# Experts' output rows added to x's rows in DRAM by the scatter, with the gate applied before the down projection

## The reference

```python
def hier_moe(x, norm_g, w_rg, b_rg, w_re, b_re, w_gate, w_up, w_down):
    hf = rmsnorm(x, norm_g).reshape(B * L, D)
    ...
    gates = jnp.sum(jax.nn.one_hot(expert_idx, N_EXPERTS, dtype=jnp.float32) * top_w[..., None], axis=1)
    y = jnp.zeros((T, D), jnp.float32)
    for e in range(N_EXPERTS):
        act = jax.nn.silu((hf @ w_gate[e]).astype(jnp.float32)) * (hf @ w_up[e]).astype(jnp.float32)
        y = y + (act * gates[:, e:e + 1]).astype(x.dtype) @ w_down[e]
    return x + y.reshape(B, L, D).astype(x.dtype)
```

## Time and profile before

| | us |
|---|---|
| median of 3 runs | 897.34 |
| lowest and highest of the runs | 894.37 and 900.54 |
| the profiled execution | 895.55 |
| its span, from the first to the last instruction | 893.7 |
| TensorE busy | 833.2 |
| VectorE busy | 614.2 |
| ScalarE busy | 464.4 |
| GpSimd busy | 263.2 |

### The profile page before, as it was taken

How to read it: one execution, slowest core, us unless ns; L and a number is a source line. 1 busy time by engine, 2 the same in 40 slices (tenths; PEclk the granted TensorE clock), 3 DMA queues, 4 the chain that set the end, 5 groups by cost and what they waited for, 6 DMA issues and landing times.

```text
span 893.7 us, 12179 instructions
## 1 busy us (share of the span) xinstructions
PE 833.2 (93%) x4237; PEld 672.5 (75%) x4237; DVE 614.2 (69%) x962; ACT 464.4 (52%) x767; POOL 263.2 (29%) x211
## 2 busy tenths in 40 slices
PE   8999999999999999999899999999999899999930
PEld 6787788878857888887577778888787588888820
DVE  4335544755677999997644454656646899999937
ACT  4523342512447888885243433451234488888722
POOL 0024991340031332231000299525101223322200
PEclk9999999999999999999899999999999999999965
DMA  8622223246818899983744222230694598999445
GB/s 279 179 75 75 71 60 95 84 127 225 354 65 350 328 330 396 397 336 126 260 115 129 67 72 83 71 118 1 193 400 184 182 406 306 381 387 382 191 149 193
DMA packets 61215, 183.67 MB, mean 206 GB/s; under 512 B 15564, under 2 KB 17868, under 8 KB 52826
## 3 DMA queue, kind: packets, MB, share of 16 engines
q1 hardware_dynamic: 46202, 147.49, 46.3%
q0 software_dynamic: 11520, 27.28, 8.8%
q10 hardware_dynamic: 3440, 8.21, 2.4%
HBM read 168.20 MB, written 29.65 MB: 221 GB/s over the span
## 4 chain that ended last, share of the span: by engine, by line
PE 85%; DVE 6%; DMA 4%; ACT 2%; issue 1%; SPq 0%; POOLq 0%; ACTq 0%
PE ps L386 14%; PE ps L390 11%; PE ps L389 11%; PE ps L1131 10%; PE ps L1133 10%; PE ps L1132 10%; PE ps L388 3%; PE ps L1138 3%; PE ps L1311 2%; PE ps L1110 2%; PE ps L1303 2%; PE ps L1243 1%; DMA back<-y_d 1%; DMA hg<-xn_d,rowidx 1%; PE ps L1268 1%
## 5 line engine op out<-in xcount | busy, mean ns | idle before, releaser
L386 PE MATMUL ps<-wh,hT 128*128 128x512 f32 x480 | 194.5, 405 | 9.1 <-DVE lT L1587 3.1
L1645 DVE TENSOR_TENSOR gul<-wgu,eh 128x1024 fp32r<-128x1024 f32 x128 | 150.7, 1217 | 6.8 <-ACT eh L878 6.7
L390 PE MATMUL ps<-wh,lT 128*128 128x512 f32 x384 | 150.5, 392 | 0.0
L389 PE MATMUL ps<-wl,hT 128*128 128x512 f32 x384 | 150.4, 392 | 0.0
L1636 DVE SCALAR_TENSOR_TENSOR wl<-raw,gcol,wh 128x512 fp32r<-128x512 f32 x80 | 75.3, 945 | 87.7 <-ACT wh L851 87.4
L878 ACT ACTIVATE eh<-wgu 128x1024 fp32r<-128x1024 f32 x128 | 128.9, 1058 | 8.3 <-PE ps L1133 6.9
L386 PEld LDWEIGHTS ps<-wh,hT 128*128 128x128 f32 x480 | 90.9, 189 | 31.8 <-issue 8.1
L1131 PE MATMUL ps<-eh,hgTh 128*128 128x512 f32 x256 | 103.3, 403 | 2.5 <-DVE hgTl L1656 2.1
L1133 PE MATMUL ps<-eh,hgTl 128*128 128x512 f32 x256 | 100.6, 393 | 0.0
L1132 PE MATMUL ps<-gul,hgTh 128*128 128x512 f32 x256 | 100.4, 392 | 0.0
L851 ACT ACTIVATE wh<-raw,gcol 128x512 fp32r<-128x512 f32 x80 | 57.7, 723 | 66.6 <-PE ps L388 49.5
(11 more groups left out here) (198 smaller groups left out, 1527.7 us busy)
## 6 DMA issues: line engine op xcount, KB each, us to landing
wgu<-in_gate_up SPq DMA_DIRECT2D x64, 1024.0 KB, 10.2
wdn<-in_w_down SPq DMA_DIRECT2D x64, 512.0 KB, 9.9
raw<-in_w_in SPq DMA_DIRECT2D x80, 256.0 KB, 2.7
raw<-in_w_out SPq DMA_DIRECT2D x32, 256.0 KB, 3.4
back<-y_d SPq DMA_DIRECT2D x16, 512.0 KB, 6.8
xn_d<-xf ACTq DMA_DIRECT2D x10, 512.0 KB, 3.7
s<-in_state_ret POOLq DMA_DIRECT2D x8, 512.0 KB, 4.8
out_new_ret_sample<-s POOLq DMA_DIRECT2D x8, 512.0 KB, 4.8
```

The lines of the kernel that those rows point to most:

```text
L386: pe.matmul(out, both, w_h, start=first, stop=False)
L389: pe.matmul(out, both, w_l, start=False, stop=False)
L390: return pe.matmul(out, l[:, t * P:(t + 1) * P], w_h, start=False, stop=final)
L1645: ve.tensor_tensor(gu_pair(gul, gul3, e, s, p), gu_pair(wgu, wgu3, e, s, p), eh[p][:, :].bitcast(F32), ALU.subtract).then_inc(glo, 1)
```

## The change

The gate is applied to the activation, before the down projection, in the same VectorE instruction that multiplies by the up half; for this the gate of each slot is needed (`gslot`), which comes out of ten small matmuls (`slot_gates`) on the gates in three bf16 parts (`gate_parts`, VectorE, once a layer, at expert 0).

x's tiles are stored to DRAM (`x_d`) once a layer by SyncE, ahead of expert 3's weights. The scatter adds its rows to those of `x_d` (`compute_op=ALU.add`) and waits for the scatter before it, as two experts may have the same token. An empty slot of partition p goes to a spare row, TOK + p, of `x_d`, so that every scatter has 128 rows in range; the gather still leaves them out. One table of indices takes the place of two.

After the last scatter SyncE loads x whole, five loads in place of ten, and `combine` is gone in both places. What waited for the sums (`x_there`) waits for the tile's load. In layer 1 the transposes of tile t+1 come before the three steps of w_in for tile t, as in layer 0. The matmuls on zeros are 38 instead of 50. SyncE's small tables and GpSimd's state load lose their wait for the sums. The branch for further turns is changed in the same manner and left out here.

```diff
@@ small tables, order of SyncE
-                if L:
-                    sp.wait_ge(comb, 2 * NT * L)
...
                 for s in range(3):
                     sp.wait_ge(gat[s], 16 * used(L, s, 0))
+                for t in range(NT):
+                    sp.wait_ge(xw, 15 * L + 2 * NT + t + 1)
+                    sp.dma_start(x_d[t * P:t * P + tokens(t), :], x[0:tokens(t), t, :]).then_inc(x_st, 16)
                 load_gu(L, AHEAD, 0)
                 load_dn(L, AHEAD, 0)
...
                 for s in range(3):
                     sp.wait_ge(y_sc[s], 16 * EUSES[s] * (L + 1))
-                for i in range(2 * NT):
-                    t, k = divmod(i, 2)
-                    n = P if t < LAST else NSAMP
-                    sp.dma_start(back[i][0:n, :], y_d[k * TOK + t * P:k * TOK + t * P + n, :]).then_inc(second_ld if i == 1 else row_ld[t], 16)
+                for t in range(NT):
+                    sp.dma_start(x[0:tokens(t), t, :], x_d[t * P:t * P + tokens(t), :]).then_inc(row_ld[t], 16)
@@ GpSimd, scatter
                 pool.wait_ge(yA, NE * L + e + 1)
                 pool.wait_ge(yV, NE * L + e + 1)
-                pool.indirect_dma_start(out=y_d, out_offset=bass.IndirectOffsetOnAxis(ap=rowidx[:, 1, e:e + 1], axis=0),
+                if e:
+                    pool.wait_ge(y_sc[(e - 1) % 3], 16 * (L * EUSES[(e - 1) % 3] + (e - 1) // 3 + 1))
+                else:
+                    pool.wait_ge(x_st, 16 * NT * (L + 1))
+                pool.indirect_dma_start(out=x_d, out_offset=bass.IndirectOffsetOnAxis(ap=rowidx[:, e:e + 1], axis=0),
                                         in_=y[s][:, :], in_offset=None,
-                                        bounds_check=2 * TOK - 1, oob_is_err=False).then_inc(y_sc[s], 16)
+                                        bounds_check=TOK + P - 1, oob_is_err=False, compute_op=ALU.add).then_inc(y_sc[s], 16)
@@ TensorE
+            def slot_gates(L):
+                pe.wait_ge(gate_in, L + 1)
+                for i in range(2 * NT):
+                    last = pe.matmul(ps[6][:, 0:3 * NE], atslot[:, i, :], gparts[:, i, :, :], start=(i == 0), stop=(i == 2 * NT - 1))
+                last.then_inc(gate_mm, 1)
...
-                if not first(e):
+                if first(e):
+                    slot_gates(L)
+                else:
                     down(L, e - 1, (s + 2) % 3)
...
-                    if t + 1 < NT and L == 0:
+                    if t + 1 < NT:
                         mix_rows(L, t + 1)
...
-                        if s == 0 and t + 1 < NT and L:
-                            mix_rows(L, t + 1)
...
-                    idle_turns(0, 50)
+                    idle_turns(0, 38)
@@ VectorE
+            def gate_parts():
+                one = both[:, :, :, :].rearrange("p k t e -> p (k t) e")
+                v = picked[:, :, :, :].rearrange("p k t e -> p (k t) e")
+                g = pgate[:, :, :].rearrange("p k t -> p (k t)").unsqueeze(2).to_broadcast([P, 2 * NT, NE])
+                link(ve.tensor_tensor(v, one, g, ALU.mult))
+                link(ve.tensor_copy(gparts[:, :, 0, :], v))
+                link(ve.tensor_tensor(v, v, gparts[:, :, 0, :], ALU.subtract))
+                link(ve.tensor_copy(gparts[:, :, 1, :], v))
+                ve.tensor_tensor(gparts[:, :, 2, :], v, gparts[:, :, 1, :], ALU.subtract).then_inc(gate_in, 1)
...
+                if first(e):
+                    ve.wait_ge(gate_mm, L + 1)
+                    link(ve.tensor_reduce(gslot[:, :], ps[6][:, 0:3 * NE].rearrange("p (i e) -> p e i", i=3), AX.X, ALU.add))
                 ve.wait_ge(silu_done, X + 1)
-                ve.tensor_tensor(act[:, :], act[:, :], ps[0][:, F:2 * F], ALU.mult).then_inc(act_done, 1)
+                ve.scalar_tensor_tensor(out=act[:, :], in0=ps[0][:, F:2 * F], scalar=gslot[:, bass.ds(e, 1)], in1=act[:, :],
+                                        op0=ALU.mult, op1=ALU.mult).then_inc(act_done, 1)
...
-                ve.scalar_tensor_tensor(out=x[0:n, t, :], in0=back[i][0:n, :], scalar=pgate[0:n, k, t:t + 1], in1=x[0:n, t, :],
-                                        op0=ALU.mult, op1=ALU.add).then_inc(comb, 1)
```

More of the change, by code:

```diff
@@ L103, in constant_tables @@
         * np.tile(valid, 2)[:, :, None],
-        "block": np.stack([P * (np.arange(2 * NT) % NT) - NO_ROW, P * np.arange(2 * NT) - NO_ROW], 1)[None] * np.tile(valid, 2)[:, :, None],
+        "block": (P * (np.arange(2 * NT) % NT) - NO_ROW)[None] * np.tile(valid, 2),
+        "spare": TOK + p[:, None],
     }
@@ L177, in build @@
         tmpf = tile("tmpf", [P, NT * NE], off=region + 4096 * 9 + 3072 + 640)
-        rowidx = tile("rowidx", [P, 2, NE], U32)
+        rowidx = tile("rowidx", [P, NE], U32)
+        gslot = tile("gslot", [P, NE])
+        gate_o = tile("gate_o", [P, 1])
         tab = region + 4096 * 3
@@ L189, in build @@
         hotturn = tile("hotturn", [P, 2 * NT, NT], off=tab + 7456)
+        aidx = tile("aidx", [P, NT * NE], U32, off=tab + 8192)
         small_tab = tile("small_tab", [P, NT * NE], off=tab + 7680)
@@ L193, in build @@
         actT = tile("actT", [P, 2, P], off=region + 4096 * 9 + 1024)
-        back = [tile(f"back{i}", [P, D], off=shared + 4096 * i) for i in range(2 * NT)]
         r12 = place(12 * 1024)
@@ L297, in build @@
         gat = [sem(f"gat{i}") for i in range(3)]
-        second_ld = sem("second_ld")
-        xn_st = [sem(f"xn_st{t}") for t in range(NT)]; upool_st = sem("upool_st"); st_st = sem("st_st")
+        xn_st = [sem(f"xn_st{t}") for t in range(NT)]; x_st = sem("x_st"); upool_st = sem("upool_st"); st_st = sem("st_st")
         s0_st = sem("s0_st"); y_sc = [sem(f"y_sc{i}") for i in range(3)]
@@ L634, in _ @@
             pool.memset(eps[:, 1:2], EPS_GN).then_inc(ready0, 1)
+            pool.memset(gate_o[:, :], 0.0).then_inc(pool_chain, 1)
+            chain[0] += 1
             pool.memset(uT[:, :], 0.0).then_inc(ready0, 1)
@@ L1414, in _ @@
                         pe.wait_ge(tab_ready, 2 * L + i // NT + 1)
-                    pe.matmul(ps[2][:, 0:2 * NE], atslot[:, i, :], over(name_p[:, i, :], 2), start=(i == 0), stop=False)
-                    last = pe.matmul(ps[2][:, 0:2 * NE], atslot[:, i, :], name_b[:, i, :, :], start=False, stop=(i == 2 * NT - 1))
+                    pe.matmul(ps[2][:, 0:NE], atslot[:, i, :], name_p[:, i, :], start=(i == 0), stop=False)
+                    last = pe.matmul(ps[2][:, 0:NE], atslot[:, i, :], name_b[:, i, :], start=False, stop=(i == 2 * NT - 1))
                 last.then_inc(tab_mm, 1)
@@ L1514, in routing @@
             ve.tensor_tensor(name_p[:, :, :], one, c("pair", 2 * NT)[:, :, 0:1].to_broadcast([P, 2 * NT, NE]), ALU.mult)
-            ve.tensor_tensor(name_b[:, :, :, :], over(one, 2, 2), c("block", 2 * NT).unsqueeze(3).to_broadcast([P, 2 * NT, 2, NE]), ALU.mult)
+            ve.tensor_tensor(name_b[:, :, :], one, c("block").unsqueeze(2).to_broadcast([P, 2 * NT, NE]), ALU.mult)
             ve.wait_ge(pos_mm, L + 1)
@@ L1528, in routing @@
             ve.wait_ge(tab_mm, L + 1)
-            ve.tensor_scalar(rowidx[:, :, :], ps[2][:, 0:2 * NE].rearrange("p (w e) -> p w e", w=2), float(NO_ROW), None, ALU.add).then_inc(tidx_done, 1)
+            ve.tensor_scalar(rowidx[:, :], ps[2][:, 0:NE], float(NO_ROW), c("spare"), ALU.add, ALU.min).then_inc(tidx_done, 1)
             ve.tensor_copy(most[:, :], most_f[:, :]).then_inc(most_done, 1)
@@ L1567, in later_turns @@
             link(ve.tensor_scalar(small_tab[:, :], tmpf[:, :], float(TOK), -float(TOK), ALU.is_ge, ALU.mult))
-            ve.tensor_tensor(tidx[:, :], small_tab[:, :], tmpf[:, :], ALU.add).then_inc(v["a"], 1)
+            link(ve.tensor_tensor(tmpf[:, :], small_tab[:, :], tmpf[:, :], ALU.add))
+            ve.tensor_scalar(aidx[:, :], tmpf[:, :], c("spare"), None, ALU.min)
+            ve.tensor_scalar(tidx[:, :], tmpf[:, :], c("spare"), None, ALU.min).then_inc(v["a"], 1)
         @block.vector
@@ L1663, in y_evac @@
                 ve.tensor_copy(y[s][:, 512:D], ps[4][:, :]).then_inc(yV, 1)
+            def gate_parts():
[7 more added lines that the diff above has]
+                ve.tensor_tensor(gparts[:, :, 2, :], v, gparts[:, :, 1, :], ALU.subtract).then_inc(gate_in, 1)
             def expert(L, e, s, n):
                 X = NE * L + e
-                if not first(e):
+                if first(e):
+                    gate_parts()
+                else:
                     dn_lo(L, e - 1, (s + 2) % 3)
@@ L1821, in _ @@
                     mix_lo(L, t)
-                    if L and t + 1 < NT:
-                        combine(L - 1, t + 1, 1)
                 if L == 0:
@@ L1916, in _ @@
                         ve.wait_ge(v["s"], i)
-                        ve.tensor_tensor(act[:, :], act[:, :], ps[0][:, F:2 * F], ALU.mult).then_inc(v["a"], 1)
+                        ve.wait_ge(v["g"], 32 * i + 16)
+                        ve.scalar_tensor_tensor(out=act[:, :], in0=ps[0][:, F:2 * F], scalar=gate_o[:, 0:1], in1=act[:, :],
```

(1 more changed line is left out.)

55 lines of the change are left out of this document (21 added, 34 removed).

## The result

The changed kernel takes 932.9 us in the median of four runs, the kernel before beside it 896.4 us: ratio 1.040, 95% interval 1.032 to 1.047. The profiled execution's span is 932.8 us against 893.7. It was predicted to be slower, at 910 us and within 878 to 926, so the time lies outside the range.

What follows compares the result with a forecast made beforehand. TensorE, busy 93% of the span, was taken as the bound, with VectorE and DMA nearly full among the experts. Terms -12.8 - 6.7 + 1 + 27.4 + 2 + 4 = +14.9 on 895.55 gave 910 us, range 878 to 926.

Steps and rivals of the forecast that it cites:

- End of the kernel: After the last scatter: without sums, the last norm ends 10.6 us after x's first landing, not 23.4; a gain of 12.8 us.
- between the layers: Between layer 0 and 1: sums before the first transposes go (2.7 us), stops between tiles hidden (4 us); gain 6.7 us.
- Gates in the product: Expert stage: the product with a gate costs 0 to 0.03 us more for each of 32 experts; gate work together +1.
- x into DRAM: Ahead of expert 3's weights: five stores, 6.1 us of DMA; no engine waits, the weights behind them move by 6.1 us.
- 13.9 us in hand: Expert stage: new DMA work per layer that fits before TensorE waits, from late weights' margin and 7.3 us idle.
- The add in the stage: Expert stage: adding scatters and x's stores take 27.6 us of DMA, 13.7 us over; stall 13.7 a layer, +27.4 in all.
- the charge by bytes: Scatters: an adding row costs DMA by its bytes, 1.049 MB a scatter; the prediction is wrong if charged otherwise.
- Two passes: Adding scatter: the old row is fetched as well as the new one written, costing DMA as much as two plain passes.
- The landing of the last scatter: After the last expert of each layer: +2 us at the end, +4 between the layers, bounds 0 and 12 together.
- The rival of the chain: Expert stage: scatters, each waiting for the one before, need over 9.3 us and set the pace; 931 us and more, chance 0.08.
- DMA not full: Sign of the chain rival: scatters released by the scatter before, over 9.3 us apart, while DMA is not full.
- The rival of the free add: Expert stage: the add costs the DMA engines nothing, so no stall; 877 to 883 us, to 888 if reads pace; chance 0.33.

Runs made afterwards that it cites:

- e6: The kernel before with x's five stores to DRAM added ahead of expert 3's weights, nothing reading them: 903.0 us, ratio 1.009.
- e8: The kernel before with x's five stores added early, ahead of SyncE's waits for router and gathers, nothing reading them: 895.7 us, ratio 0.999.
- e1: The changed kernel with experts reordered so neighbours share no token, each scatter waiting only for the one four back: 910.5 us, ratio 1.017.
- e3: The changed kernel with empty slots out of range again, so an adding scatter moves 72 rows, not 128: 930.7 us, ratio 1.040.
- e5: The changed kernel with both the reordered experts of e1 and the 72 rows of e3: 910.3 us, ratio 1.017.
- e7: e5 with x's stores issued early, before SyncE waits for the router and the gathers: 899.1 us, ratio 1.003.
- e2: The changed kernel with the scatter's add struck out, so rows of x are overwritten; wait and 128 rows kept: 884.7 us, ratio 0.987.
- e4: The kernel before with one thing added, each plain scatter waiting for the one before: 896.3 us, ratio 1.000.
- e13: The changed kernel, experts in own order and scatters chained, with empty slots out of range, early stores and rows balanced over the engines: 884.2 us, ratio 0.986.
- e12: e7 with the rows balanced over the DMA engines, four or five on each: 878.5 us, ratio 0.981.

## Why the prediction was wrong

*End of the kernel, between the layers.* Right at the end: -13.4 for -12.8. Between the layers -5.6 for -6.7, but divided otherwise. Up to the first matmul with w_in only 0.4 us went where 2.7 were forecast: the first read of x landed 6.4 us after its issue, that of before 3.7 us. GpSimd's load of the retention state now falls into the same microseconds (0.40 MB on its queue from 459 to 468 us), which the prediction had "not on the path"; how much of the 2.7 us is its doing isn't shown. From there to the first square 5.1 us went where 4 were forecast. Gates in the product cost 0.48 us where the plain product took 0.41, so 2.1 us for 32 experts, where at most 0.03 us each were allowed; too small to matter.

*x into DRAM.* "No engine waits for them; the weights behind them move by 6.1 us" was the step that failed here. The 13.9 us in hand were read from the last weights of the stage and handed to the first. e6 puts the price at 7.9 us for both layers, e8 at zero for another place.

*The add in the stage.* +13.7 a layer was forecast, +10.3 and +8.5 came, and without the wait +14.6 and +13.1 (e1). The size is near, but that is luck. The forecast was a stall by late weights alone; in layer 0 about 7 of the 10.3 us came from the buffers of `y`, that is from the chain. And the charge by bytes is wrong, which the prediction named as what would undo it: 128 rows or 72, the time is the same (e3, e5), since the fullest engines have eight rows in both. "Two passes" is right for a single row, 328 against 159 ns. The rule of the Trainium skill ("Collectives: The Full Stack", Part 3), told there of ReduceScatter, that an add needs two source reads and so halves the rate, agrees with this factor of 2.06; that two reads are its cause no run shows. The 13.9 us in hand were an average over sixteen engines, while by the counts above the work falls mostly on eight. What these eight have in hand stays open: in e7, 11 scatters with eight rows of 169 ns more each are 14.9 us for 9.7 us of stall, an estimate of 5 us in hand; by the whole transfer (3.58 against 1.33 us) it would be 25 us of work and 15 in hand.

*The landing of the last scatter.* This is the main error: +6 us were forecast, +37.5 came. The failed sentence is "Within the stage there are 9.3 us between them", taken as enough on the strength of landings in quiet. Under load an adding scatter took 10 to 15 us, so that GpSimd fell back by about 2 us an expert, and behind the last down projection three scatters were left, each 6.0 us and nearly a microsecond of issue. That the cause is the wait together with the add is shown: without the wait the tails are 8.0 and 7.6 us (e1), without the add 7.6 and 6.6 (e2), and the wait on plain scatters costs nothing (e4). The rival of the chain had this mechanism, its condition and even the time (931 us), but let the whole delay fall on TensorE through the buffers of y, 24 us a layer. Some 7 us of it did, and the rest came out as a tail; so the agreement of 931 with 932.9 us is partly luck too. Its sign "DMA not full" did not hold either, the share being 1.03. It had a chance of 0.08. The rows to weigh it by were at hand: gathers landing after 8.5 us, and a second pass to be added.

The rival of the free add is answered by e2, 884.7 us: that is what the change takes, with its late stores and 128 rows, when the scatter doesn't add.

## What to carry to other kernels

A transfer that must wait for its predecessor is to be priced by its landing under load, not in quiet, and compared with the pace of the loop; if it is above, look for the delay first in the buffers that the transfer holds and then in the tail. DMA idle time averaged over sixteen engines isn't slack: ask which engines the rows of a partly filled tile go to, and whether the idle time lies before the tightest deadline. Spreading the rows of an indirect transfer over the engines was a change of one constant here. The order made by the engine rule paid; the one that spread the rows evenly over the partitions did nothing.

## What the runs showed of the hardware

- Most 4 KB rows of an adding indirect transfer take 328 ns on their DMA engine, of a plain one 159 ns (quiet scatters of the changed kernel and of the one before), and the first ones of an adding transfer up to 1500 ns. In quiet 128 adding rows land after 6.0 us (67 in the first slots after 6.1, e3), 67 or 64 plain ones after 4.1 or 3.2; balanced, 56 to 96 adding rows land after 4.7 to 5.4 (e13).
- A scatter with up to 64 valid rows in the first slots uses eight of the sixteen engines, by the rule and by the rows in flight (eight, as long as it lasts, for the 64 rows of the last scatter before); for the gather it is the rule alone. The balanced order took the landing of weights under load from 23.6 to 10.6 us (e7, e12).
- Some issues of indirect transfers take 4.1 to 6.8 us on GpSimd's timeline instead of 1 to 3.2, in every kernel here, from one of them (the kernel before) to eleven (e6); their cause wasn't looked for.
